# A residual stack on one NeuronCore: input-projection units spread further into the attention slots, output-projection units begun before attention ends

## The reference

```
h = rmsnorm(x); proj = h @ w_in               # 1024 -> 2304 = 18 tiles of 128
a_q,a_k,a_v, b_u,b_v, c_q,c_k,c_v = split(proj)   # 3+3+3, 2+2, 3+1+1 tiles
y_a = diff attention(a_q,a_k,a_v)   # 6 heads, two softmaxes each: p0 - lam*p1, then rmsnorm per head
y_b = b_u * (w_s @ layernorm(b_v) + b_s)          # "gmlp", mixing tokens in chunks of 128
y_c = window attention(c_q,c_k,c_v) # 6 heads over 2 kv heads, blocks of 128, window 128, sinks
x = x + rmsnorm(concat(y_a,y_b,y_c) @ w_out)      # 1024 -> 1024 = 8 tiles
```

## Time and profile before

| | us |
|---|---|
| three timed runs | 3506.68, 3505.32, 3504.80; median 3505.32 |
| profiled execution, its own time | 3504.89 |
| its span in the trace | 3503.1 |
| PE busy in the span | 3352.9 (96%) |
| POOL / DVE / ACT busy | 1625.6 / 1209.4 / 1162.8 |
| attention slots of layer 0, from first scores to last weighing | 68.08 to 228.70 |
| of layer 1 | 789.19 to about 949.9 |

### The profile page before, as it was taken

How to read it: one execution, slowest core, us unless ns; L and a number is a source line. 1 busy time by engine, 2 the same in 40 slices (tenths; PEclk the granted TensorE clock), 3 DMA queues, 4 the chain that set the end, 5 groups by cost and what they waited for, 6 DMA issues and landing times.

```text
span 3503.1 us, 42736 instructions
## 1 busy us (share of the span) xinstructions
PE 3352.9 (96%) x15456; PEld 2743.6 (78%) x15456; DVE 1209.4 (35%) x1774; ACT 1162.8 (33%) x1760; POOL 1625.6 (46%) x838
## 2 busy tenths in 40 slices
PE   8989999989899999899999989999999999899998
PEld 6777888777678887788887767888888888578887
DVE  4533114445421144511344532114411443421133
ACT  4733223437342233422232153223322333222222
POOL 6725444556264445644454315444544453144443
PEclk9989999989899999899999989999999999999998
DMA  4102222221022222232222102222222222112221
GB/s 150 51 25 90 96 96 96 72 95 54 13 90 96 96 96 79 93 108 96 96 84 101 68 13 85 96 97 98 95 96 97 98 92 84 43 64 104 96 96 60
DMA packets 80360, 293.90 MB, mean 84 GB/s; under 512 B 8923, under 2 KB 9435, under 8 KB 79996
## 3 DMA queue, kind: packets, MB, share of 16 engines
q1 hardware_dynamic: 78912, 286.19, 23.3%
q10 hardware_dynamic: 1340, 6.23, 0.5%
HBM read 290.28 MB, written 2.10 MB: 83 GB/s over the span
## 4 chain that ended last, share of the span: by engine, by line
PE 90%; DVE 3%; POOL 3%; issue 2%; ACT 2%; DMA 0%; POOLq 0%; DVEq 0%; SPq 0%; ACTq 0%
PE bank L1604 27%; PE bank L1606 27%; PE bank L1605 27%; PE bank L1873 2%; POOL diag L605 1%; PE bank L1854 1%; PE bank L1834 1%; PE bank L1649 1%; PE bank L1779 1%; PE bank L1631 1%; PE bank L1802 0%; POOL w_lo L521 0%; ACT y L815 0%; DVE mvl L1080 0%; PE bank L2024 0%
## 5 line engine op out<-in xcount | busy, mean ns | idle before, releaser
L521 POOL TENSOR_TENSOR w_lo<-w_raw,w_hi 128x1024 fp32r<-128x1024 f32 x537 | 1313.6, 2449 | 1617.4 <-ACT w_hi L677 1617.2
L1604 PE MATMUL bank<-mvh,w_hi 128*128 128x512 f32 x4296 | 1701.9, 396 | 51.2 <-DVE mvl L1080 44.3
L1606 PE MATMUL bank<-mvh,w_lo 128*128 128x512 f32 x4296 | 1681.7, 391 | 0.0
L1605 PE MATMUL bank<-mvl,w_hi 128*128 128x512 f32 x4296 | 1681.6, 391 | 0.0
L677 ACT ACTIVATE w_hi<-w_raw 128x1024 fp32r<-128x1024 f32 x537 | 568.6, 1060 | 1908.6 <-PE bank L1606 1905.5
L1604 PEld LDWEIGHTS bank<-mvh,w_hi 128*128 128x128 f32 x4296 | 812.9, 189 | 245.1 <-DVE mvl L1080 42.7
L1606 PEld LDWEIGHTS bank<-mvh,w_lo 128*128 128x128 f32 x4296 | 812.3, 189 | 171.9
L1605 PEld LDWEIGHTS bank<-mvl,w_hi 128*128 128x128 f32 x4296 | 813.5, 189 | 168.3 <-issue 3.4
L1152 DVE TENSOR_TENSOR scr<-bank,rstd_b 128x512 f32<-128x512 f32 x264 | 181.3, 691 | 995.0 <-PE bank L1606 994.8
L1169 DVE TENSOR_TENSOR mvl<-big,mvh 128x512 fp32r<-128x512 f32 x132 | 269.3, 2051 | 347.3 <-ACT mvh L751 347.3
L605 POOL TENSOR_TENSOR diag<-diag,scr 128x512 f32<-128x512 f32 x105 | 146.7, 1397 | 36.0 <-ACT scr L697 29.5
(11 more groups left out here) (171 smaller groups left out, 1543.7 us busy)
## 6 DMA issues: line engine op xcount, KB each, us to landing
w_raw<-in_weights SPq DMA_DIRECT2D x537, 512.0 KB, 3.2
x<-in_x SPq DMA_DIRECT2D x4, 512.0 KB, 9.4
out_y<-y SPq DMA_DIRECT2D x4, 512.0 KB, 2.7
tab<-in_dist ACTq DMA_DIRECT2D x2, 640.0 KB
tab<-in_gmlp ACTq DMA_DIRECT2D x2, 640.0 KB
tab<-in_ret_dil ACTq DMA_DIRECT2D x1, 1280.0 KB
y<-in_p ACTq DMA_DIRECT2D x2, 512.0 KB, 3.4
y<-in_rotary ACTq DMA_DIRECT2D x1, 1024.0 KB
```

The costliest lines, as they stand in the source:

```text
L521: nc.gpsimd.tensor_tensor(w_lo[:, slot, :], w_raw[:, slot, :], w_hi[:, slot, :].bitcast(F32), ALU.subtract).then_inc(w_lo_ready, 1)
L1604: nc.tensor.matmul(bank[:, :], hi, mvh[:, k, :], start=first, stop=False)
L1605: nc.tensor.matmul(bank[:, :], hi, mvl[:, k, :], start=False, stop=False)
L1606: return nc.tensor.matmul(bank[:, :], lo, mvh[:, k, :], start=False, stop=last)
```

## The change

* The last nine units of `a_in` are computed in another order (A_TILES): BV, CQ, CK, CV first, BU last; the weights are stored in that order, and `evacuate` writes tile A_TILES[s]. PLACE gives the unit of a tile for the waits.
* WORK gives products per slot, before and after the even pair's transposes: (3, 2) in slots 0 to 7, (2, 2) in slots 8 to 15, none in slots 16 to 19, (1, 1) in slots 20 to 24. The first 72 are a_in's; the last ten are k 0 to 4 of a_out's units 0 and 1, in banks 2 and 3. UNIT_SLOT follows: units 9 to 17 end in slots 1, 3, 4, 6, 7, 9, 11, 13, 15.
* MISC becomes bank 7; window scores use banks 0 and 1 only and are issued in their own slot; odd window pairs are transposed into bank 6.
* In window slots pair p - 1 is weighed after the transposes of pair p (before: p - 2).
* gmlp statistics move to slots 5 and 6, the power to 6, normalisation to 7 and 8, scale and shift to 9 and 10. Adding the bias stays in 13 and 14 (`gmlp_mixed`), the gating is its own step in slots 15 and 17, and the halves follow in 16 and 18.
* The last differential block is normalised in slot 15 (was 16); DIFF_OUT is 16 to 18 (was 17 to 19); SWA_ON 16, 19, 22; SWA_OUT 19, 21, 23.
* The tail begins with the last weighing, then unit 2 and unit 3 (k 0 to 4), then the rest as before. `scale` of `emit` falls away; it was always None.

```diff
-OUT, MISC = 5, 3
-BACK_A = SCORE + (2, 3, 4, 5)
+OUT, MISC = 5, 7
+BACK_A = (2, 3, 0, 1, 4, 5, 6, 7)
+A_TILES = tuple(range(9)) + (11, 12, 13, 14, 15, 16, 17, 9, 10)
...
-                self.banks = SCORE if self.diff else SCORE[2 * (n % 2):2 * (n % 2) + 2]
+                self.banks = SCORE if self.diff else SCORE[0:2]
...
-        UNIT_SLOT = {s: (8 * (s - 8) - 1) // 6 for s in range(9, 18)}
-        UNIT_EARLY = {s: (8 * (s - 8) - 1) % 6 < 3 for s in range(9, 18)}
-        AV_SLOT = {5: 3, 6: 4, 13: 5}
+        WORK = [(3, 2)] * 8 + [(2, 2)] * 8 + [(0, 0)] * 4 + [(1, 1)] * 5
+        FIRST = [sum(a + b for a, b in WORK[:n]) for n in range(len(WORK) + 1)]
+        UNIT_SLOT, UNIT_EARLY = {}, {}
+        for s in range(9, 18):
+            last = 8 * (s - 8) - 1
+            UNIT_SLOT[s] = max(n for n in range(SLOTS) if FIRST[n] <= last and sum(WORK[n]))
+            UNIT_EARLY[s] = last < FIRST[UNIT_SLOT[s]] + WORK[UNIT_SLOT[s]][0]
+        PLACE = {m: s for s, m in enumerate(A_TILES)}
+        VT_SLOT = {3: 3, 4: 4, 13: 5}
         DIFF_TAKE = {4: 0, 7: 1, 10: 2, 13: 3}
-        DIFF_ON = {6: 0, 9: 1, 12: 2, 16: 3}
-        DIFF_OUT = {17: 0, 18: 1, 19: 2}
-        SWA_ON = {17: 0, 20: 1, 23: 2}
-        SWA_OUT = {20: 0, 22: 1, 24: 2}
+        DIFF_ON = {6: 0, 9: 1, 12: 2, 15: 3}
+        DIFF_OUT = {16: 0, 17: 1, 18: 2}
+        SWA_ON = {16: 0, 19: 1, 22: 2}
+        SWA_OUT = {19: 0, 21: 1, 23: 2}
         MIX = {13: 0, 14: 1}
-        A_ORDER = ["g0", "g1", "d0", "d1", "d2", "w0", "w1", "w2", "w3"]
+        GATE = {15: 0, 17: 1}
+        A_ORDER = ["d0", "g0", "d1", "d2", "g1", "w0", "w1", "w2", "w3"]
...
-            return banks[4 if p < DIFF_PAIRS or p % 2 == 0 else 2]
+            return banks[4 if p < DIFF_PAIRS or p % 2 == 0 else 6]
...
+            def gmlp_mixed(l, g):
+
+                dve.wait_ge(mixed_done, 2 * l + g + 1)
+                nc.vector.tensor_tensor(gtmp[:, g, :].rearrange("p (b c) -> p b c", c=P),
+                                        banks[MISC][:, :].rearrange("p (b c) -> p b c", c=P),
+                                        tab[:, 1024 + g * P:1024 + (g + 1) * P].unsqueeze(1).broadcast_to([P, TB, P]),
+                                        ALU.add).then_inc(mix_taken, 1)
+
             def gmlp_gate(l, g):
+                dve.wait_ge(mix_taken, 2 * l + g + 1)
+                dve.wait_ge(bank_free, lin[f"a_in{l}"].e0 + PLACE[BU + g] + 1)
                 nc.vector.tensor_tensor(gtmp[:, g, :], gtmp[:, g, :], big[:, BU + g, :],
                                         ALU.mult).then_inc(gated_ready, 1)
...
-                if n < DIFF_GROUPS:
+                if n < len(GROUPS):
                     scores(n)
-                elif n == DIFF_GROUPS:
-                    scores(n)
-                    scores(n + 1)
-                elif n + 1 < len(GROUPS):
-                    scores(n + 1)
...
                 for p in (even, odd):
                     transpose_probs(p)
-                    if p == DIFF_PAIRS:
-                        weigh_values(p - 1)
-                    elif p > DIFF_PAIRS + 1:
-                        weigh_values(p - 2)
+                    products(p % 2)
+                    weigh_values(p - 1)
+
+            def partial(l, i, k0, k1):
+
+                out = lin[f"a_out{l}"]
+                if k0 == 0:
+                    pe.wait_ge(w_lo_ready, out.u0 + i + 1)
+                    if i < 2:
+                        pe.wait_ge(bank_free, lin[f"a_in{l}"].e0 + 17 + i)
+                for k in range(k0, k1):
+                    if i == 0 and k < 5:
+                        pe.wait_ge(mv_lo, moved(l, ("d0", "d1", "d2", "g0", "g1")[k]) + 1)
+                    last = three(banks[BACK_A[i]], (out.u0 + i) % RING, k, k, k == 0, k == KT - 1)
+                if k1 == KT:
+                    last.then_inc(unit_done, 1)
...
                 pe.wait_ge(a_scaled, ITEMS * (l + 1))
-                pe.wait_ge(mv_lo, moved(l, "w0"))
-                partial(0, 0, 5)
-                last_values(PAIRS - 2)
-                last_values(PAIRS - 1)
-                partial(1, 0, 5)
-                pe.wait_ge(mv_lo, moved(l, "w3"))
+                pt_ready(pe, l, p)
...
+                partial(l, 2, 0, 5)
+                pe.wait_ge(mv_lo, moved(l, "w2") + 1)
                 transpose_out(w_block(l, TB - 1), [banks[MISC]], 3, onorm[:, 1:2, :])
-                partial(2, 0, 5)
-                partial(3, 0, 5)
+                partial(l, 3, 0, 5)
                 pe.wait_ge(mv_lo, moved(l, "w3") + 1)
                 for i in range(RING):
-                    partial(i, 5, KT)
+                    partial(l, i, 5, KT)
                 for i in range(RING, KT):
-                    partial(i, 0, KT)
+                    partial(l, i, 0, KT)
```

More of the change, by code:

```diff
@@ L155, in program, with window_cat @@
         o_raw = scr[:, 9, 0:64 * DIFF_H]
+        def window_cat(part, b):
+            return part[:, 5:8, b * P:(b + 1) * P]
         diff_out = [big[:, 18 + b, 0:64 * DIFF_H] for b in range(TB)]
@@ L632, in _ @@
                 splits(a.u0 + 9 + RING)
-                for n in range(DIFF_GROUPS + 3):
+                for n in range(max(UNIT_SLOT.values()) + 1):
                     attention_slot(l, n)
@@ L1190, in emit, with window_low @@
                 at = (slice(None), slice(tile0, tile0 + tiles), slice(b * P, (b + 1) * P))
[L1191 to L1195, removed]
+                nc.vector.tensor_tensor(mvl[at], src, mvh[at].bitcast(F32), ALU.subtract).then_inc(mv_lo, 1)
+            def window_low(l, b):
+                dve.wait_ge(mv_hi, moved(l, f"w{b}") + 1)
+                nc.vector.tensor_tensor(window_cat(mvl, b), banks[MISC][:, 0:3 * P].rearrange(
+                    "p (a b) -> p a b", b=P), window_cat(mvh, b).bitcast(F32), ALU.subtract).then_inc(mv_lo, 1)
             def turn(a, t):
@@ L1543, in _ @@
                 window_normalised(l, TB - 1)
-                emit(moved(l, "w3"), w_block(l, TB - 1), TB - 1, banks[MISC], 5, 3, None)
+                window_low(l, TB - 1)
                 rstd_ready(f"a_out{l}")
@@ L1666, in from_x @@
                     for j in range(min(k, RING)):
-                        product(j, k)
+                        of_x(j, k)
                     if k < RING:
@@ L1875, in weigh_values, with products @@
                     last.then_inc(a_pv, 1)
-                def products(n0, n1):
-                    for i in range(n0, n1):
+                def products(half):
+                    n0 = FIRST[n] + (WORK[n][0] if half else 0)
+                    for i in range(n0, n0 + WORK[n][half]):
                         s, k = 9 + i // 8, i % 8
+                        if s > 17:
+                            partial(l, (i - 72) // 5, (i - 72) % 5, (i - 72) % 5 + 1)
+                            continue
                         if k == 0:
@@ new lines, in attention_tail @@
+            def attention_tail(l):
+                p = PAIRS - 1
+                g, e = pair(p)
+                h = g.heads[e]
+                pe.wait_ge(a_scaled, ITEMS * (l + 1))
+                pt_ready(pe, l, p)
+                nkb = g.kb1 - g.kb0
+                for i in range(nkb):
+                    last = nc.tensor.matmul(banks[OUT][:, h * 64:(h + 1) * 64], ptile[:, p % 2, i * P:(i + 1) * P],
+                                            g.value(e, g.kb0 + i), start=(i == 0), stop=(i == nkb - 1))
+                last.then_inc(a_pv, 1)
+                partial(l, 2, 0, 5)
+                pe.wait_ge(mv_lo, moved(l, "w2") + 1)
```

149 lines of the change are left out of this document (63 added, 86 removed).

## The result

The changed kernel takes 3460.78 us (median of 4 runs, 3460.42 to 3461.91) against 3505.06 us for the kernel before in the same comparison (3503.49 to 3506.68): ratio 0.9874, 95% interval 0.9857 to 0.9891. That is 44 us less, where 31 were predicted.

What follows compares the result with a forecast made beforehand. PE, busy 90% of the span, bounds the kernel; only its idle or low-clock time can be won. Per layer -10.9 - 1.4 (slots 12 to 24) - 6.8 + 1.0 + 2.5 = -15.6 us, two layers -31: 3474 us, range 3462 to 3492.

Steps and rivals of the forecast that it cites:

- Slots 0 to 11: Differential attention: 16 a_in products leave each layer, -10.9 us, with 1.0 us back for POOL lateness that pushes ACT.
- Rival A: Differential slots stay at 7.98 us, held by ACT or POOL; 10.9 us a layer stays, 3496 us; chance 0.10.
- Slots 12 to 15: First window slots: gmlp wait of 5.84 us goes, PE with four products a slot sets the time, 25.8 us.
- Slots 16 to 19: Window slots without products: DVE-ACT loop of 4.2 us a slot stays, plus gmlp operations and normalisation, 19.4 us.
- such meetings: Shared port: moved gmlp operations meeting a POOL split in slot 15 cost DVE 0 to 2.1 us; taken as 0.
- Slots 20 to 24: Last window slots, two a_out products each: PE work sets 19.7 us, and the 7.10 us slot 20 goes.
- Rivals B: Window slots: products add to the loop; slots 12 to 24 take 78.2 us, not 64.9; about 3490; chance 0.14.
- D: Clock falls in slot 16, not back before slot 24, moved products at 1.2 GHz; 3525 us; chance 0.04.
- The clock, +2.5: Low PE clock in slots 16 to 19 costs 2.5 us a layer, bounds 0 and +8.
- The tail: After slot 24, where PE is full: ten a_out products fewer, -6.8 us a layer.
- rival E: No clock loss and no POOL loss; 3467 us or a little less; chance 0.12.
- rival C: Half clock in all of slots 16 to 19; +5.5 us a layer over the forecast, 3485 us; chance 0.15.

Runs made afterwards that it cites:

- s3: s2 with 16 a_in products a layer moved from slots 0 to 11 into slots 12 to 15; 3469.49 us, 0.9898 to the kernel before.
- s5: s2 with the old order back: pair p-2 weighed behind pair p's transposes, block normalisation one slot later; 3490.23 us, 0.9961 to the kernel before.
- s6: Kernel before with only pair p-1 weighed behind pair p's transposes and block normalisation one slot earlier; 3490.51 us, 0.9956.
- s9: Changed kernel with weighing and block normalisations put back as in s5, all moved products kept; 3470.43 us, 0.9908 to the kernel before.
- second profile: Kernel before and changed kernel each run once more, unedited; 3504.94 us (0.9997) and 3464.36 us (0.9890).
- s1: Changed kernel with its slot structure alone: a_in and a_out products and gmlp chain back at their old slots; 3492.82 us, 0.9967 to the kernel before.
- s2: s1 with the gmlp chain moved three slots up; 3477.96 us, 0.9921 to the kernel before.
- s7: Changed kernel with the gmlp chain two slots later, as in the kernel before, products still spread; 3475.45 us, 0.9911 to the kernel before.

## Why the prediction was right in its mechanism and short in its size

The miss is 13 us: spans differ by 44.1, the sum said 31. By its own steps, in us a layer (layer 0, layer 1):

- *Slots 0 to 11*: predicted -9.9 (10.9 of products, 1.0 back for GpSimd and ACT), measured -10.0 and -10.1. Right in both terms: s3 shows it alone (84.2 us), and slot 11 is 1.0 us longer than slots 8 to 10, by the way that the prediction names: GpSimd pushes ACT, for whose late copies PE waits. Rival A is out.
- *Slots 12 to 15*: predicted 25.8, measured 25.96 and 25.98. Right, slot by slot 6.2, 8.5, 6.3 and 5.0 for 6.4, 7.8, 6.4 and 5.2; slot 13 has a wait of 0.94 us for ACT's copy of the transposed values, and I had 0.4 for waits.
- *Slots 16 to 19*: predicted 19.4, measured 18.45 and, at clock 0.91, 19.61. The loop that I named sets slots 17 to 19. In slot 16 it is the normalised output, through DVE's addition beside GpSimd's split. I took 0 for such meetings, because PE's slot would cover them. In slot 16 it did not: 1.0 us more of wait, 0.3 us net, since slot 17 is shorter by the rest.
- *Slots 20 to 24*: predicted 19.7, measured 19.07 and 19.09, all PE work. Rivals B and D are out. The order of the weighing, on which the reason given there rests, is what s5, s6 and s9 test. It was the largest thing in the structure: 12 to 15 us in all without moved products, 6 to 10 with them. The prediction had it only within its sum and did not put a price on it.
- *The clock, +2.5*: this is the step that failed. Measured are 0 and 1.2, and 0 and 2.1 in the second profile, 0.8 in the mean. I read a share of low clock from the kernel before (0.80 and 0.82 over the stretch) and charged part of it to slots 16 to 19. But in layer 0 of that kernel the low clock lay elsewhere, around the waits of slot 13 and from slot 20 on. The 28 us between, with scores, transposes, 64-column matmuls and one of the gmlp products, were at 1.00. In layer 1 slots 16 to 19 had 0.90. Layer 0:

```profile
178.00:206.00 28.00, 21.39 (x161) 16.20 (x161) 17.84 (x49) 14.32 (x41) 2.57 (x5) 1.00 0.00 1
```

The change takes the long wait out of slot 13, puts products in place of idle time in slots 12 to 15, and leaves no wait in slots 20 to 24 (s1 and s2, without a product there and with waits of at most 0.9 us, had 1.00 too). None, one or two low stretches are left. And slots 17 to 19 are bound by DVE and ACT at 4.2 us and more, so part of a low clock there costs nothing; the 1.2 us is what shows through. Predicted 5.0 in the two layers, 1.2 in this pair: 3.8 of the 13.

- *The tail*: predicted -6.8, measured -7.8 and -7.7. The ten products are the 6.8. What I priced at nothing are the weighings: the kernel before has two of them in this stretch, together 0.8 us (232.35 to 233.16 in its trace), the changed kernel none. The remaining 0.1 to 0.2 is the first product, which in the kernel before still runs partly at the low clock. 1.9 us of the 13.
- *Outside the layers*: predicted 0, measured -3.9 in this pair of profiles, and +2.0 in the second pair (3090.3 and 3092.3). No effect, so these 4 us of the 13 are luck of the pair. On another chip the changed kernel took 3464.36 us (ratio 0.9890), so on which side of 3462 the time falls is within this scatter. That it lies some 10 us under 3474 is not.

The rest is 3.2 us by which slots 16 to 24 at full clock (37.5 a layer) lie under my 39.1, 0.3 in slots 0 to 11, and 0.3 back in slots 12 to 15. Together 12.8 of 13.1. The time is nearest to rival E (3467 "or a little less"), which had 0.12, but not by E's reason: the loss on GpSimd came as forecast, and the clock loss in one layer of two. E took only the two loss terms off the sum, and nothing lower was in the terms. What the range lacked is the scatter of the places that are not changed (up to 5 us) and a low side for the slot sums.

The sentence that transposes do not count as PE activity in the usual way (the Trainium skill, TensorE: Matmul & The Clock Gate, Part 4: PE-mode transpose) led to rival C, half clock in slots 16 to 19. Here it did not come about: those slots, scores, transposes and 64-column matmuls only, had 14.63 us of PE work in 18.45 at granted clock 1.00. The stretch at 0.50 that I had called agreement is one side of the trace before; the 28 us shown above are the other. The measurement decides: a stretch of that kind may keep its 2.4 GHz.

## What to carry to other kernels

Full work on both sides of a stretch with idle PE is worth moving into it, and its price there can be read: ten products cost 3.3 us where they had cost 6.8. But take the waits of the stretch first, each with its own price, for they were worth more: one order of two lines in PE's queue (weighing one pair earlier, so that a block's last pair, the normalisation and the next block's first pair do not meet in one slot) brought 12 to 15 us before the products moved, the gmlp chain 15, and all 52 moved products 17. Look where in a stretch the low clock lies before you carry a share of it over: here it stood behind waits that the change removes. And when work moves, look at what its helpers on other engines will meet: with the a_in products a weight split on GpSimd moved into slot 16, and PE's wait there became 1.0 us longer.

## What was not expected of the hardware

The low clock moves about between executions of one kernel: slots 16 to 19 of the changed kernel had 1.00 and 0.91 in the two layers of one execution, and the same kernel ran layer 1 in 186.1 and 187.0 us. It also stayed at 1.00 without any product (slots 20 to 24 of s1: 13.04 us busy of 15.36, scores, transposes and 64-column matmuls). Where it fell, PE had mostly stood during or just before: 4.96 and 6.15 us for GpSimd in slot 13 of s7 and s1, 1.08 and 1.11 in slot 12 of s2, 1.18 and 2.14 in slot 17 of s5, 1.64 in slot 16 of the changed kernel. Before the fall in slot 16 of s6 there was no wait over 0.73 us. And the same wait of 1.64 us was followed by no fall in two layers of eight, and that of 2.28 us in slot 23 of s5 by none in layer 0 and by one in layer 1, so the runs give no rule for it.

In every layer of the changed kernel's two profiles, of s3 and of s7, a 128 x 6 addition on DVE took 1.2 us beside a GpSimd weight split, and 0.16 in the later slots without one.
